# The modulation rows of the first phase in four column groups of TensorE, in a two-layer RG-LRU and GLA step

## The reference, cut to what matters

```python
def ada_mod(cvec, w, b):
    m = jax.nn.silu(cvec) @ w + b
    return m.reshape(-1, 1, N_MOD, D_MODEL)

def modulated(x, mod, gains, j):
    return rms_norm(x, gains[j]) * (1.0 + mod[:, :, 3 * j + 1]) + mod[:, :, 3 * j]

def half_ffn(x, mod, gains, j, w_in, w_out):
    return x + FFN_RES * mod[:, :, 3 * j + 2] * swiglu(modulated(x, mod, gains, j), w_in, w_out)
```

## Time and profile before

| | us |
|---|---|
| median of 3 runs | 1554.78 |
| all runs | 1553.71, 1554.78, 1556.09 |
| span of the profiled execution, first to last instruction | 1553.2 |

### The profile page before, as it was taken

How to read it: one execution, slowest core, us unless ns; L and a number is a source line. 1 busy time by engine, 2 the same in 40 slices (tenths; PEclk the granted TensorE clock), 3 DMA queues, 4 the chain that set the end, 5 groups by cost and what they waited for, 6 DMA issues and landing times.

```text
span 1553.2 us, 24614 instructions
## 1 busy us (share of the span) xinstructions
PE 1518.0 (98%) x8774; PEld 1479.9 (95%) x8774; DVE 1128.2 (73%) x1717; ACT 661.7 (43%) x956; POOL 185.4 (12%) x279
## 2 busy tenths in 40 slices
PE   9999999999979999999999999999989999999998
PEld 5999999989979999999999999998779999999998
DVE  5898888878987877688887777986977475444432
ACT  4433342369965433332343333325555454333321
POOL 0001000001240000001000000000794000000000
PEclk9999999999989999999999999999999999999999
DMA  9576676623423656677555666763222134334421
GB/s 384 185 253 216 230 242 218 201 68 108 151 96 109 213 183 194 198 228 232 171 179 186 191 189 214 250 196 113 68 82 77 61 109 149 122 128 141 152 93 41
DMA packets 68279, 257.04 MB, mean 165 GB/s; under 512 B 7584, under 2 KB 8608, under 8 KB 67968
## 3 DMA queue, kind: packets, MB, share of 16 engines
q1 hardware_dynamic: 48944, 187.57, 36.1%
q0 software_dynamic: 18512, 67.58, 13.5%
q10 hardware_dynamic: 768, 1.19, 0.2%
HBM read 253.68 MB, written 2.63 MB: 165 GB/s over the span
## 4 chain that ended last, share of the span: by engine, by line
PE 85%; DVE 7%; ACT 3%; POOL 2%; issue 1%; DMA 1%; SPq 0%; DVEq 0%; ACTq 0%; POOLq 0%
PE bank L557 26%; PE bank L559 25%; PE bank L558 25%; DVE tmp_a L1570 2%; DVE h_lo L1589 1%; DMA ada_first<-in_ada_w 1%; ACT w_hi_sb L1009 1%; PE wide L862 1%; DVE w_lo_sb L1482 1%; PE bank L656 1%; PE bank L570 1%; PE bank L884 0%; DVE bcum L2053 0%; ACT rgs L1261 0%; PE bank L901 0%
## 5 line engine op out<-in xcount | busy, mean ns | idle before, releaser
L1009 ACT ACTIVATE w_hi_sb<-raw 128x1024 fp32r<-128x1024 f32 (+3 forms) x308 | 344.1, 1122 | 477.3 <-PE bank L559 450.9
L557 PE MATMUL bank<-h_hi,w_hi_sb 128*128 128x384 f32 x1567 | 529.1, 338 | 2.3 <-ACT vt L1452 1.0
L1482 DVE TENSOR_TENSOR w_lo_sb<-raw,w_hi_sb 128x1024 fp32r<-128x1024 f32 (+3 forms) x308 | 403.3, 1310 | 170.3 <-ACT w_hi_sb L1009 167.0
L558 PE MATMUL bank<-h_lo,w_hi_sb 128*128 128x384 f32 x1567 | 526.6, 336 | 0.0
L559 PE MATMUL bank<-h_hi,w_lo_sb 128*128 128x384 f32 x1567 | 526.6, 336 | 0.0
L557 PEld LDWEIGHTS bank<-h_hi,w_hi_sb 128*128 128x128 f32 x1567 | 294.6, 188 | 6.4 <-DVE h_lo L1589 2.1
L558 PEld LDWEIGHTS bank<-h_lo,w_hi_sb 128*128 128x128 f32 x1567 | 294.6, 188 | 0.0
L559 PEld LDWEIGHTS bank<-h_hi,w_lo_sb 128*128 128x128 f32 x1567 | 294.6, 188 | 0.0
L557 PE MATMUL bank<-a_hi,w_hi_sb 128*128 128x384 f32 x704 | 236.8, 336 | 1.5 <-DVE a_lo L1704 1.5
L559 PE MATMUL bank<-a_hi,w_lo_sb 128*128 128x384 f32 x704 | 236.6, 336 | 0.0
L558 PE MATMUL bank<-a_lo,w_hi_sb 128*128 128x384 f32 x704 | 236.5, 336 | 0.0
(11 more groups left out here) (314 smaller groups left out, 1640.1 us busy)
## 6 DMA issues: line engine op xcount, KB each, us to landing
raw<-in_ffn_in SPq DMA_DIRECT2D x176, 512.0 KB, 3.8
ada_raw<-in_ada_w POOLq DMA_DIRECT2D x128, 512.0 KB, 3.7
raw<-in_ffn_out SPq DMA_DIRECT2D x64, 704.0 KB, 4.4
raw<-in_rg_in SPq DMA_DIRECT2D x20, 512.0 KB, 3.8
ada_first<-in_ada_w SPq DMA_DIRECT2D x8, 1024.0 KB, 19.1
raw<-in_rg_out SPq DMA_DIRECT2D x8, 640.0 KB, 3.9
raw<-in_gla_qk SPq DMA_DIRECT2D x8, 512.0 KB, 4.3
raw<-in_gla_v SPq DMA_DIRECT2D x8, 512.0 KB, 3.4
```

What stands on the lines that cost most here:

```text
L557: pe.matmul(out, w_hi_sb[:, slot, w], hi[k], start=start and j == 0, stop=False)
L558: pe.matmul(out, w_hi_sb[:, slot, w], lo[k], start=False, stop=False)
L1009: A(w_hi_sb[:, s, 0:w], raw[:, s, 0:w], ACT.Copy).then_inc(w_hi, 1)
L1482: V.tensor_tensor(w_lo_sb[:, s, 0:w], raw[:, s, 0:w], w_hi_sb[:, s, 0:w].bitcast(F32), ALU.subtract).then_inc(w_split, 1)
```

## The change

The stationary operand of a row is padded to 32 columns (two of silu values, thirty of zeros, cleared once by GpSimd), and contraction step j writes to partitions 32(j mod 4) to 32(j mod 4) + 31 of the bank, so that four partial sums of two steps each stand in four groups of 32 partitions. The copy takes all 128 partitions. The turning matmul contracts over all 128 with a 0/1 matrix `fold` (a new input of two columns in `small`) in place of the identity, and thereby adds the four partial sums. The tensor `csil` moves to the memory behind `ada_first`.

```diff
-                  ("gla_b", 2 * HEADS), ("gla_g", DC), ("wz", DC * 2 * RANK), ("ident", P)]:
+                  ("gla_b", 2 * HEADS), ("gla_g", DC), ("wz", DC * 2 * RANK), ("ident", P), ("fold", 2)]:
...
-        csil = sb("csil", [P, DC, 2])
...
         ada_first = sb("ada_first", [P, ADA_START, DC * P], F32, first_scope)
+        csil = sb("csil", [P, DC, 32], F32, first_scope)
...
+            pool.memset(csil[:, :, :], 0.0).then_inc(csil_cleared, 1)
             pool.memset(ones[:, :], 1.0).then_inc(consts, 1)
...
                 for j in range(DC):
-                    last = pe.matmul(mod_bank[n % 2][0:2, 0:2 * P], csil[:, j, :], w[:, 2 * P * j:2 * P * (j + 1)],
-                                     start=j == 0, stop=j == DC - 1)
+                    g = slice(32 * (j % 4), 32 * (j % 4) + 32)
+                    last = pe.matmul(mod_bank[n % 2][g, 0:2 * P], csil[:, j, :], w[:, 2 * P * j:2 * P * (j + 1)],
+                                     start=j < 4, stop=j >= 4)
...
                     last = pe.matmul(mod_bank[n % 2][:, 2 * P + 2 * c:2 * P + 2 * c + 2],
-                                     ada_first[0:2, 2 * k, c * P:(c + 1) * P], ident[0:2, 0:2], start=True, stop=True)
+                                     ada_first[:, 2 * k, c * P:(c + 1) * P], fold, start=True, stop=True)
...
-                A(ada_first[0:2, 2 * k, 0:2 * P], mod_bank[n % 2][0:2, 0:2 * P], ACT.Copy).then_inc(row_copied, 1)
+                A(ada_first[:, 2 * k, 0:2 * P], mod_bank[n % 2][:, 0:2 * P], ACT.Copy).then_inc(row_copied, 1)
...
                 act.wait_ge(small_loaded, 16)
-                A(csil[:, :, :], csm, ACT.Silu).then_inc(csil_ready, 1)
+                act.wait_ge(csil_cleared, 1)
+                A(csil[:, :, 0:2], csm, ACT.Silu).then_inc(csil_ready, 1)
...
+             "fold": (np.arange(P)[:, None] % 32 == np.arange(2)[None, :]).astype(np.float32)}
```

More of the change, by code:

```diff
@@ L243, in build @@
         ident = sm("ident")
+        fold = sm("fold")
         s0 = ada_raw[:, :, :].rearrange("p a b -> p (a b)").rearrange("p (h d v) -> p h d v", h=HEADS, d=2)
@@ L266, in build @@
         ada_used = sem("ada_used")
+        csil_cleared = sem("csil_cleared")
         csil_ready = sem("csil_ready")
@@ L2245, in lay_out @@
              "h0": cols(i["state_rglru"][0, 0]), "gla_b": cols(i["gla_b_g"][0]), "gla_g": cols(i["gla_norm"][0]),
-             "wz": wz, "ident": np.eye(P, dtype=np.float32)}
+             "wz": wz, "ident": np.eye(P, dtype=np.float32),
+             "fold": (np.arange(P)[:, None] % 32 == np.arange(2)[None, :]).astype(np.float32)}
     o["small"] = c_(np.concatenate([parts[k].reshape(P, -1) for k in SMALL], axis=1))
```

## The result

| us | before | after |
|---|---|---|
| median of 20 runs each | 1554.30 | 1557.33 |
| lowest and highest run | 1553.47, 1556.42 | 1551.91, 1562.37 |
| profiled execution, its own time | none given | 1556.41 |
| span of the profiled execution | 1553.2 | 1554.7 |

One disturbed run of after (1863.34 us, at a mean granted clock of 0.747) counts in the median of 20 only; the median of the other 19 is 1556.56 us. Its other single runs differ by 10.5 us, those of before by 3.

The account below looks back on a forecast made before the run. TensorE was taken as the bound, busy 1518.0 of 1553.2 us. Row 7's 1.5 us off the span gives 1551.7; with the median 1.6 us above the span, the forecast was 1553.3 us, range 1552.0 to 1556.0.

Parts of the forecast that it names:

- Bounds of the first phase: Up to 50.79 us: gains in rows 0, 1, 2, 4 and 6 are lost in waits; block 3 starts 1.51 us earlier.
- row 7 is the one that pays: Row 7 still starts at 40.14 us but ends at 42.17, not 43.68; its turn and block 3 move 1.51 us.
- The small edits: Wider copy, larger turning matmul and clear of csil: taken as nothing; the copy bounded by 0.13 us, the clear by 0.4.
- The price of a row: Each modulation row's sixteen records overlap partly and take 2.03 us, 1.51 us less; forecast chance 0.46.
- the lower bound: A row with all four column groups fully beside each other: four rounds, three steps and 0.30, or 0.95 us.
- four groups truly side by side: Rival for the rows, chance 0.20: full overlap of column groups gains 1.59 us, a median of 1553.2 us.
- the cap: At row 7's turn: ScalarE's copy allows it no earlier than 43.87 us, so 1.59 us is the most gain.
- the exposed loads: Rival, chance 0.07: padded weight loads not hidden, a row takes 4.9 to 6.6 us, kernel ends at 1558.9 to 1564.0.
- The clock: Rival, chance 0.04: rows that end sooner leave TensorE idle in the first phase, and its clock falls.
- one loss to the clock: Case of the clock falling once, put at 1554.8 us, the same as no overlap; falling twice was left out.
- no DMA and no other engine sets TensorE's pace: Behind 50.79 us, where block 3 starts: time taken out of the first phase reaches the kernel's end, 1.51 us.

Follow-up runs that it names:

- the change again: The changed kernel run and profiled once more with no edit: median 1562.98 us, ratio 1.0039 against the kernel before.
- short rows with the old places: The kernel before with two of each row's eight contraction steps, no column groups, csil in its place: 1555.08 us, ratio 1.0003.

## Why the prediction was right or wrong

**Bounds of the first phase: right up to row 7.** Rows 0 to 2 are worth nothing; row 4 starts at 28.31 us (forecast 28.45), released by its transfer; row 6 at 33.43 (33.48), by its transfer; `part(3)` waits for h_lo(3) and goes at 37.56 (37.64); `turn_row(6)` waits for the copy, at 39.31 (39.60); row 7 is the one that pays. That `turn_row(7)` at 44.07 (43.95) and block 3 at 49.20 (49.28) agree so well is luck: `part(4)` started 1.46 us behind row 7's start, not 2.03, and then took 2.76 us, not 1.78, at the lower clock. The small edits that lie in the first phase (128 partitions in the copy, the larger turn, the clear) cost nothing that reaches row 4.

**The price of a row: mis-sized.** The step was "the second record of one group runs beside the first of the next", eight steps, 2.03 us. The starts of row 4's sixteen records, in us:

```
28.310 28.317 28.324 28.330 | 28.550 28.557 28.564 28.570
28.766 28.773 28.780 28.786 | 28.982 28.989 28.995 29.002
```

Four start 7 ns apart and the next four 0.24, then 0.216 us after them: the four rounds of the lower bound, 0.69 us to the last start in place of 15 x 0.216 = 3.24. The rival "four groups truly side by side" holds, fp32's two records for each matmul or not. ScalarE's copy, which was to cap the gain at 1.59 us, did not end it in this execution: `copy_row(7)` ended at 43.44 us, 0.63 us ahead of `turn_row(7)`, which had to follow the slow `part(4)` on TensorE:

```profile
43.08 0.36 ACT L1035 ACTIVATE ada_first<-bank 128x256 f32<-128x256 f32 x1
```

With the waits filled and the clock full it did, and there the cap was higher, with block 3 1.76 us earlier than before:

```profile
43.79 0.61 PE L670 MATMUL bank<-small,ada_first 128*128 128x2 f32 x4 [0.79 <-ACT ada_first L1054]
...
49.03 0.34 PE L561 MATMUL bank<-h_hi,w_hi_sb 128*128 128x384 f32 x1
```

The weight loads stayed hidden: line 660 has sixteen of 110 ns for each row, 1.76 us together, and a row takes 1.07 us, with four starts within 20 ns. So the exposed loads, the one rival on the slower side, did not come.

**The clock: a rival undersold.** It had 0.04. The waits that it names, about 1.4 and 1.1 us, are shorter than the 2.7 us ahead of the 0.56 in the earlier trace rows, and whether it falls was judged by the longest single wait. But the change thinned the whole of the first phase: from 10 to 50.8 us TensorE was busy for 31.7 of 40.8 us (14.90 + 16.78), before for 39.3 (18.53 + 20.80). No wait that ends in a row above is longer than 1.31 us, the longest of the whole phase is 2.05 us:

```profile
12.55 0.62 PE L669 MATMUL bank<-small,ada_first 128*128 128x2 f32 x4 [2.05 <-ACT ada_first L1035]
```

The granted clock was 0.83 and 0.92 all the same, and where `part(4)` runs it was half of full speed, 0.50 from 41 to 43 us: steps of 0.32 us. The forecast's range takes 1554.8 us for one loss to the clock, the whole gain; no row and no run shows that term by itself. In its place the runs showed a loss that differs: in the change again, at 0.50 from 36 to 45 us, block 3 started at 50.86 us and the gain was gone; in the execution of after the fall on the path came later and left 1.59 us of gain. The ratios go the same way, with intervals that overlap: short rows with the old places came out at 1.0003, the change with the old places at 0.9999, and with the waits filled at 0.9990.

**What made it slower: a step that failed.** The forecast said that behind 50.8 us "no DMA and no other engine sets TensorE's pace", and so it is; but it took TensorE's own pace, 173 ns for a matmul, as given. And under "the small edits" the diff's line that moves `csil` was costed not at all, as if a declaration were no part of the time. It shifted `h_hi` and the tensors behind it by 56 bytes, as declared, against the weights, and by the table that went with steps of 176.5 ns in place of 173.4. Of the 4.0 us (3.3 by the median of the other 19 runs) between the median and the forecast, the places cost the most: with them restored the same change measured 1554.23 us, 0.9 from the forecast. That this rest is the clock's loss is argued: it is of that size.

**What stays open.** Why the distance between the moving operands and the weights costs 6 ns at every other matmul (174 and 180 ns by turns in place of 173 and 174); why at 56 and at 64 bytes it does so in some stages only, and in the change not in the same ones in both executions, while at 128 bytes it did in all eight stages; whether another distance than those run here is better than that of before, since none below 173.3 ns was seen. What decides whether one execution of the change keeps its clock was seen only as the clock of each run.

## What to carry to other kernels

When a small edit adds, moves or removes a tensor, hold the places of everything behind it (a pad of the same size), or the comparison measures the layout as well (`csil` moved alone: 1563.15 us against 1554.18); and where a kernel is bound by a steady loop, compare the count of matmuls in the same 50 us before and after, because the longer step showed neither in the busy share nor in the waits (285 in place of 290, with 50.00 us busy in both). Four column groups made rows of fp32 matmuls with two output columns 3.4 times as short (1.07 us in place of 3.62); how much of it reaches the end is read from what else arrives at that time. The phase that was thinned out lost the clock for work that was not touched (0.83 and 0.92 in place of 1.00), and 40 matmuls on constants in the waits held it from 30 us on (1.00 in place of 0.91); what that is worth at the end has to be measured.

## What the runs showed of the hardware that was not expected

With the moving operands 128 bytes further from the weights than before, as declared, the mean step of the long matmuls was 176.7 ns in all eight stages in place of 173.3, and the kernel 1.45% slower; from 802 to 852 us the granted clock was 1.00 and TensorE busy for all 50.00 us. With 256 bytes nothing was lost (173.3 to 173.6 ns, ratio 0.9998). fp32 matmuls in four column groups started 7 ns apart. And the clock fell, to 0.83 and 0.92, in a phase in which TensorE never stood for more than 2.05 us.
